# Wider gather blocks in a streaming MoE layer: three expert pairs to a block, one output column group per fill

## What is computed

```
for l in range(DEPTH):                      # 2 layers
    mix = hybrid_mixer(x, mem, ...)
    x = layer_norm(ALPHA * x + mix, ln1_g[l], ln1_b[l])
    top_idx, top_w = route(x, ...)          # 8 of 64 experts for each token
    y = sum over e: top_w * (silu(x @ w_gate[e]) * (x @ w_up[e])) @ w_down[e]
    x = layer_norm(ALPHA * x + y + swiglu(x, ws_gate, ws_up, ws_down), ln2_g[l], ln2_b[l])
```

## Time and profile before

| | us |
|---|---|
| median of 3 runs | 1224.52 (1223.61 to 1224.72) |
| the profiled execution, whole time | 1223.63 |
| its span, first to last instruction | 1221.7 |
| PE busy in the span | 1181.2 (97%) |
| DVE, ACT busy | 351.0 (29%), 262.0 (21%) |
| DMA | 452.45 MB, 370 GB/s over the span |

### The profile page before, as it was taken

How to read it: one execution, slowest core, us unless ns; L and a number is a source line. 1 busy time by engine, 2 the same in 40 slices (tenths; PEclk the granted TensorE clock), 3 DMA queues, 4 the chain that set the end, 5 groups by cost and what they waited for, 6 DMA issues and landing times.

```text
span 1221.7 us, 17928 instructions
## 1 busy us (share of the span) xinstructions
PE 1181.2 (97%) x7776; PEld 560.6 (46%) x7776; DVE 351.0 (29%) x1070; ACT 262.0 (21%) x509; POOL 10.4 (1%) x20
## 2 busy tenths in 40 slices
PE   7999899999999999999899999999999999999994
PEld 6764444444444444444386645344444443444431
DVE  0433632222222222222243337222222222222224
ACT  0132222221222212222112323122221222212210
POOL 0000000000000000000010000000000000000001
PEclk9999999999999999999999999999999999999998
DMA  9962299999999999999997415999999999999992
GB/s 384 421 285 83 87 392 430 427 426 428 427 427 426 426 428 428 426 427 426 422 387 308 192 35 206 399 429 427 428 426 427 427 428 428 427 426 426 429 427 107
DMA packets 35927, 452.45 MB, mean 370 GB/s; under 512 B 3969, under 2 KB 4097, under 8 KB 6529
## 3 DMA queue, kind: packets, MB, share of 16 engines
q1 hardware_dynamic: 35840, 451.22, 88.0%
HBM read 450.15 MB, written 1.05 MB: 369 GB/s over the span
## 4 chain that ended last, share of the span: by engine, by line
PE 89%; DMA 7%; DVE 2%; ACT 0%; POOL 0%; issue 0%; SPq 0%; POOLq 0%
PE bank L611 33%; PE bank L637 17%; PE bank L529 8%; PE bank L554 5%; PE bank L693 5%; PE bank L765 4%; DMA slots<-in_w_gu 3%; DMA slots<-in_w_dn 3%; PE bank L702 2%; PE bank L623 2%; PE bank L892 1%; PE bank L712 1%; PE bank L578 1%; PE bank L722 1%; PE bank L667 1%; PE bank L661 1%
## 5 line engine op out<-in xcount | busy, mean ns | idle before, releaser
L637 PE MATMUL bank<-slots,low 128*32 128x512 f32 x2048 | 233.0, 595 | 2.9 <-issue 1.7
L611 PE MATMUL bank<-slots,low 128*64 128x512 f32 x1024 | 226.5, 594 | 2.4 <-DMA slots<-in_w_gu 2.4
L611 PE MATMUL bank<-slots,xT 128*64 128x512 f32 x1024 | 226.1, 594 | 1.0 <-ACT xT L927 1.0
L1194 DVE SCALAR_TENSOR_TENSOR yparts<-bank,small,yparts 128x512 fp32r<-128x512 f32 x128 | 96.1, 751 | 249.7 <-ACT yparts L927 249.7
L529 PEld LDWEIGHTS bank<-high,low 128*128 128x128 bf16 x1536 | 108.2, 147 | 50.4 <-issue 49.7
L611 PEld LDWEIGHTS bank<-slots,low 128*64 128x64 f32 x1024 | 69.1, 137 | 132.4 <-issue 127.6
L611 PEld LDWEIGHTS bank<-slots,xT 128*64 128x64 f32 x1024 | 69.3, 137 | 130.6 <-issue 129.3
L927 ACT ACTIVATE yparts<-bank,small 128x512 fp32r<-128x512 f32 x128 | 88.0, 687 | 158.5 <-PE bank L637 158.5
L1186 DVE TENSOR_TENSOR high<-high,bank 128x256 f32<-128x256 f32 x64 | 26.9, 421 | 327.3 <-ACT high L949 327.3
L529 PE MATMUL bank<-high,low 128*128 128x128 bf16 x1536 | 117.7, 227 | 0.3
L637 PEld LDWEIGHTS bank<-slots,low 128*32 128x32 f32 x2048 | 60.6, 109 | 121.9 <-issue 116.6
(11 more groups left out here) (128 smaller groups left out, 664.3 us busy)
## 6 DMA issues: line engine op xcount, KB each, us to landing
slots<-in_w_gu SPq DMA_DIRECT2D x128, 2048.0 KB, 23.7
slots<-in_w_dn SPq DMA_DIRECT2D x64, 2048.0 KB, 23.2
slots<-in_dense SPq DMA_DIRECT2D x32, 1024.0 KB, 13.0
r<-in_pool_mat SPq DMA_DIRECT2D x2, 1024.0 KB, 23.6
r<-in_ln_g SPq DMA_DIRECT2D x4, 512.0 KB, 4.6
r<-in_ln_b SPq DMA_DIRECT2D x4, 512.0 KB, 5.6
slots<-in_shared_dn SPq DMA_DIRECT2D x2, 1024.0 KB, 4.9
low<-in_memt SPq DMA_DIRECT2D x2, 512.0 KB, 6.8
```

What stands on the lines that cost most here:

```text
L611: m = pe.matmul(H[64 * a:64 * a + 64, :], xg[B % 2][:, k, j, a, :], GU[g][:, a, :, k, :], start=k == 0, stop=k == KD - 1)
L637: m = pe.matmul(Y[half][r0:r0 + 32, :], hT[:, kc * P + 64 * a + 32 * t:kc * P + 64 * a + 32 * t + 32], DN[g][:, a, kc, half * 512:(half + ...
L1194: dve.scalar_tensor_tensor(ysp[:, 1, half * 512:(half + 1) * 512], Y[half][:, :], wslot[:, b:b + 1], ysp[:, 0, half * 512:(half + 1) * 512 ...
```

## The change

- A gather block is three pairs (`SPAN` = 3): 11 blocks, the last of two pairs. A fill is one output column group k (of 8): six matmuls of 192 columns (128 in the last block), each written as one run. Block B + 1 is filled in 3, 3 and 2 fills in the three pairs of block B. The third fill of a pair stands between the two halves of the down product (L637 before).
- ScalarE's copy of a fill is 384 columns (256 in the last block), and reads them in another order than they lie: token tile and place are swapped back during the copy.
- The first block of a layer takes 8 fills, 48 matmuls of 192 columns; fills 4 to 7 reuse banks 4 to 7 after ScalarE's copy of fills 0 to 3.
- `xg` now needs 3072 columns for each of its two buffers. The even one lies in the scratch area; the odd one lies in a joined tensor `xr` (`xT` and `r8`), and covers the first 1024 columns of `r8`. So the `ln2` loads are issued no longer before pair 2's weights but after the loop, once pair 29 has used the odd buffer, and ahead of the next layer's memt.
- `hT`, `pos` and `w3` move to memory that is free in the loop.

```
+SPAN = 3
+BLOCKS = -(-PAIRS // SPAN)
+WIDTH = [min(SPAN, PAIRS - SPAN * b) for b in range(BLOCKS)]
+FILLS = KD
...
-                sp.wait_ge(*x_at(l, 0, NT - 1))
-                norms(l, ln2_g, ln2_b)
                 sp.wait_ge(*full_at(l, "sh1"))
                 load_gu(main, l, 2, 2)
...
+                sp.wait_ge(main.h_full, l * PAIRS + PAIRS - 2)
+                norms(l, ln2_g, ln2_b)
...
-            def gather(ps, B, quarter, buf, to=G):
-
-                for kk in range(2):
-                    k = 2 * quarter + kk
-                    for t in range(NT):
-                        for s in range(3):
-                            m = pe.matmul(to[:].rearrange("p (k x t c) -> p k x t c", k=2, x=4, t=NT)[:, kk, :, t, :],
-                                          xsp[:, t, s, k::KD], sel[:, buf, t, :].rearrange("p (x c) -> p x c", x=4),
-                                          start=s == 0, stop=s == 2)
+            def gather(ps, B, k, buf, to=G):
+
+                x = 2 * WIDTH[B]
+                for t in range(NT):
+                    for s in range(3):
+                        m = pe.matmul(to[:, t * x * SLOTS:(t + 1) * x * SLOTS], xsp[:, t, s, k::KD], sel[:, buf, t, 0:x * SLOTS],
+                                      start=s == 0, stop=s == 2)
                 m.then_inc(ps.g_full, 1)
...
-                for f in range(4):
-                    gather(ps, first_block, f, 0, bank[4 + f])
-                pe.wait_ge(ps.g_sb, first_fill + 1)
+                for f in range(FILLS):
+                    if f >= 4:
+                        pe.wait_ge(ps.g_sb, first_fill + f - 3)
+                    gather(ps, 0, f, 0, bank[4 + f % 4])
+                pe.wait_ge(ps.g_sb, first_fill + 5)
...
+                    ks = [k for k in range(SPAN * j, SPAN * j + SPAN) if k < FILLS and filling]
...
                         m.then_inc(ps.y_full, 1)
+                        if half == 0 and len(ks) > 2:
+                            pe.wait_ge(ps.g_sb, fills + ks[2])
+                            gather(ps, B + 1, ks[2], (B + 1) % 2)
...
+                def g_fill(B, k, src=G):
+                    act.wait_ge(ps.g_full, first_fill + FILLS * B + k + 1)
+                    x = 2 * WIDTH[B]
+                    dst = xg[B % 2][:, k, 0:WIDTH[B]].rearrange("p r e (t c) -> p (r e) t c", t=NT)
+                    copy(dst, src[:, 0:NT * x * SLOTS].rearrange("p (t x c) -> p x t c", t=NT, x=x)).then_inc(ps.g_sb, 1)
```

More of the change, by code:

```diff
@@ L199, in build @@
         rt = pT[:, 0, :]
-        memT = [mixT, xT[:]]
+        memT = [mixT, xT]
         def prob_of(c):
@@ L208, in build @@
         off[0] -= NT * D
[L209 to L212, removed]
+        xg_even = part(KD * SPAN * P)
         off[0] += 2 * D + 2 * P
@@ L215, in build @@
         sg = part(2 * F).rearrange("p (t n) -> p t n", t=NT)
-        sel = part(2 * NT * P // 2, BF16).rearrange("p (b t c) -> p b t c", b=2, t=NT)
-        pos = part(NT * E)
+        sel = part(2 * NT * SPAN * 64 // 2, BF16).rearrange("p (b t c) -> p b t c", b=2, t=NT)
+        w3 = sg[:, 1, 0:NT * E * 3 // 2].bitcast(BF16).rearrange("p (t e s) -> p t e s", t=NT, s=3)
+        hT = sw[:, 0:2 * F]
+        pos = sw[:, 2 * F:2 * F + NT * E]
         off[0] = NT * 3 * D // 2 + D + KD * 2 * P
@@ L538, in turn_sel @@
                 gb = G[:].bitcast(BF16)
-                half = sel[:, q // 2 % 2, :, 64 * (q % 2):64 * (q % 2) + 64]
+                half = sel[:, q // SPAN % 2, :, 64 * (q % SPAN):64 * (q % SPAN) + 64]
                 for t in range(NT):
@@ L617, in body @@
                         pe.wait_ge(ps.selT_sb, n + 1)
-                        gather(ps, first_block + B + 1, 2 * j, (B + 1) % 2)
+                        gather(ps, B + 1, ks[0], (B + 1) % 2)
                     if not first:
@@ L625, in body @@
                     if filling:
-                        pe.wait_ge(ps.g_sb, fills + 1)
-                        gather(ps, first_block + B + 1, 2 * j + 1, (B + 1) % 2)
+                        pe.wait_ge(ps.g_sb, fills + ks[1])
+                        gather(ps, B + 1, ks[1], (B + 1) % 2)
                     pe.wait_ge(ps.w_in[2][g], (turn * USES[g] + use) * 16 + 16)
@@ L937, in run @@
                 base = turn * PAIRS
-                first_fill = turn * 4 * BLOCKS
-                def g_quarter(B, quarter, src=G):
-                    act.wait_ge(ps.g_full, first_fill + 4 * B + quarter + 1)
-                    dst = xg[B % 2][:, 2 * quarter:2 * quarter + 2].rearrange("p k r e s -> p (k r e s)")
-                    copy(dst, src[:, :]).then_inc(ps.g_sb, 1)
-                for f in range(4):
-                    g_quarter(0, f, bank[4 + f])
+                first_fill = turn * FILLS * BLOCKS
+                def g_fill(B, k, src=G):
[3 more added lines that the diff above has]
+                    copy(dst, src[:, 0:NT * x * SLOTS].rearrange("p (t x c) -> p x t c", t=NT, x=x)).then_inc(ps.g_sb, 1)
+                for f in range(FILLS):
+                    g_fill(0, f, bank[4 + f % 4])
                 def body(n, q, g, b, use, first, last):
+                    B, j = q // SPAN, q % SPAN
+                    ks = [k for k in range(SPAN * j, SPAN * j + SPAN) if k < FILLS and B + 1 < BLOCKS]
                     act.wait_ge(ps.h_full, n + 1)
                     act.activation(sg[:, 0, :], H[:, 0:F], ACT.Silu).then_inc(ps.silu_rd, 1)
-                    if q // 2 + 1 < BLOCKS:
-                        for f in range(2):
-                            g_quarter(q // 2 + 1, 2 * (q % 2) + f)
+                    for k in ks[0:2]:
+                        g_fill(B + 1, k)
                     act.wait_ge(ps.selT_sb, n + 1)
@@ L957, in body @@
                             .then_inc(ps.hi_rd, 1)
+                        if half == 0:
+                            for k in ks[2:]:
+                                g_fill(B + 1, k)
                 pairs_of_pass(base, body, 0, (lambda: load_count(act, l)) if round_ is None else None)
```

36 lines of the change are left out of this document (18 added, 18 removed).

## The result

The changed kernel takes 1232.05 us (1231.14 to 1233.13) against 1224.07 us (1223.58 to 1224.72) for the kernel before in the same comparison: a ratio of 1.0066, with a 95% interval of 1.0054 to 1.0078. The forecast of 1229.1 was 3 us short and the time lies just above the range of 1226.2 to 1231.8; slower was right, but in part by luck, as is said at the end of the point-by-point part. The profiled execution took 1232.54 us, its span was 1230.6, 8.9 more than before.

What follows compares the result with a forecast made beforehand. The DMA stream at 427 GB/s, 14.7 us a pair, was taken to bound the loops, not PE. First block 0.95 + 0.95 plus loads 2.7 made +4.6 us on 1224.5, so 1229.1 us, range 1226.2 to 1231.8.

Steps and rivals of the forecast that it cites:

- Part 1: Gathers inside the expert loop: 16 wide matmuls at 83 ns save PE about 0.3 us per pair, worth nothing on the path.
- 8 ns in a matmul at most: Loop gathers: writing contiguous columns instead of four runs of 32 saves at most 8 ns per matmul.
- Part 2: First block's gather ahead of pair 0: 48 wide matmuls, less a shorter last copy, net +0.95 us in each layer.
- The rival of slow permuted copies: First block: ScalarE's copies take 0.75 us instead of 0.5, giving +9.3 us, 1233.8; chance 8%.
- Part 3: Moved ln2 loads ahead of layer 1's dense: 2.9 us less 0.2 slack stalls L661, +2.7 us; hidden after layer 1.
- A later pair 0 is a later end, one for one: Loop start: the DMA stream starts with pair 0, so any delay of pair 0 delays the loop's end equally.
- The clock rival: Pairs from 22 on: PE's waits drop its clock to 1.2 GHz, giving 1240 us or more; chance 2%.
- The rival in which PE's pace counts: Expert loops: if the stream had room, filling pairs give 18 us, less the 4.6, so 1211; chance 5%.
- the waits from pair 22: Sign in the loop: from about pair 22 PE waits about 1.2 us per pair for w_gu and w_dn.
- the wait at the dense chunk: Sign after the loop: L661 of layer 1 waits nearly 3 us for the dense load.
- A: Post-measurement theory, loop: DMA held the kernel before by only 1.4 to 2.1 us a layer; finer cutting of PE's work costs more.
- B: Post-measurement theory, stream: the first block and moved norm loads delay the DMA stream; PE's slower pair is a side effect.

Runs made afterwards that it cites:

- the fused one: Changed kernel with the third fill's six matmuls directly behind the second's, in another PSUM bank, down product whole: 1226.79 us, ratio 1.0020.
- the two versions of the changed kernel with a fast PE: Changed kernel with the third fill's matmuls and copy left out, 1224.66 us; changed kernel with the third fill right behind the second, 1226.79 us.

## Why the prediction was right or wrong, point by point

**What bounds the kernel before: right, but with too little said of the margin.** The prediction said that PE's pace "has no more say once it is at or below 14.7 us a pair". A faster PE gives nothing (the kernel without the third fill; the fused one), and the 427 GB/s held in each kernel. But the bound of 14.7 is for an endless stream. PE starts with a lead and must be slower by only a little, over 30 pairs, for its own sum to end last: the waits at pair 31, worth 1.4 and 2.1 us, are the whole margin of a layer, 0.05 to 0.07 us per pair. A pair of 14.04 us, well below 14.7, was already too slow. The prediction had these numbers and used them for one direction only.

**Part 1: this step failed.** "PE gains about 0.3 us per pair, at most 0.4" rested on 16 x 83 ns, and no bound of it reached below zero; measured is a loss of 0.18. With it fell "It is worth nothing on the path": the loops lost 6.05 us where the sum has no term. Column time was right: back to back, a wide matmul takes 84 ns (4.05 us / 48 in the first block) for the 83 assumed. What was left out is what goes with a group. The fused kernel shows 12 in one group at 90 ns each (1.08 / 12), the changed one 6 at 109 to 122. Taking six out of the twelve costs 0.30 us: 0.15 for the group inside the down product, and 0.07 and 0.07 for a wait and the start behind it, since six before the down product cover less of VectorE's copy than twelve did. The prediction named that last effect, without a price. Cutting the down product adds 0.13. Why a group inside the down product takes 0.15 us more than one behind the transposes no run here separates. In a pair with three fills: 0.64 + 0.73 + 0.65 + 0.13 = 2.15 us, against 1.70 before, +0.45, as the chain's 14.31 for 13.86. In a pair with two: 0.64 + 0.72 = 1.36, less 0.34. Twice the one and once the other are +0.56 over three pairs, +0.18 a pair. The forecast average of 16 matmuls a pair was right, but it hid that two pairs of three pay for the third group. Nor is their width the cause: the kernel before with one quarter cut loses 0.54 us a pair with narrow matmuls.

**The layout, "8 ns in a matmul at most": wrong.** The saving from contiguous columns is none at 128 columns, by the kernel that writes in one run. The 62 ns of the earlier trace rows is the price of a 128-column matmul here in either layout.

**Part 2, the first block: right.** +0.92 and +0.91 for +0.95: the 48 matmuls take 159.81 to about 163.9, 4.05 us, and the last copy is shorter. The rival of slow permuted copies is refuted; ScalarE's copy of 384 columns takes 0.49 us (its timeline, changed kernel: duration after start):

```profile
160.51 3.96 ACT L933 ACTIVATE low<-bank 128x384 f32<-128x384 f32 x8 [5.37 <-PE bank L530]
...
172.29 0.49 ACT L933 ACTIVATE xr<-bank 128x384 f32<-128x384 f32 x1 [0.25 <-PE bank L530]
```

The first row also shows what the sum did not say: the eight copies run back to back, 0.495 us each, level with PE's fills of 0.506, and the chain of waits goes over the copies to pair 0. By that chain, slower copies would have lengthened this stretch; no run has them.

**Part 3, the loads: mechanism right, term mis-sized, and not on the path in the end.** "The slack is 0.2 us" was 1.2, because records were counted as matmuls; so the term is 1.75 in the kernel before, from start to start, and 1.1 to 1.15 in the two versions of the changed kernel with a fast PE. In the changed kernel itself it is zero, since PE comes to L667 after the data: the stretch is 143.96 us for 143.97.

**"A later pair 0 is a later end, one for one": right for a large shift, not seen for small ones.** Later by 3.0 came out as 2.9 a layer. Earlier by 0.6 came out as no gain in time. DMA had moved 403 GB/s for 400 in the 40 us from L578, about 0.3 us of stream. The landing of the last half scatters by about 1 us between kernels whose pair 0 starts alike (443.5 and 443.6 us after L578 in the kernel before, 444.5 and 443.3 with the gathers in one run), and with pair 0 later by 0.9 it came 0.3 earlier to 1.7 later. So shifts below 1 us can't be followed to the end in single traces, and whether something holds the stream besides pair 0 was not settled. In the changed kernel this does not matter: there pair 0's 0.9 us lie on PE's own path.

**The rivals.** The clock rival is refuted where its condition held: in the kernel without the third fill, with PE waiting up to 1.2 us per pair, PEclk is 1.00, that is 2.4 GHz, over 200 to 590. The rival in which PE's pace counts was close to the truth with the wrong sign. None of the rivals had PE slower inside the loop at the full clock, though the change cuts PE's work into more groups; that missing case is why the range ended at 1231.8. Of the signs named, the rate, the first block's 4 us and the copy came true; the waits from pair 22, the wait at the dense chunk and the late w_gu of pair 31 did not appear in the changed kernel. In the two versions with a fast PE the waits came later than pair 22 (from pair 24 and 23 without the third fill, from pair 28 of layer 0 with the fused one), the dense chunk did stall PE, and the last w_gu was late in three layers of four.

**What explains the 8.0 us.** A, with B's small part: 1.8 ahead of pair 0 and 6.05 in the loops, where 4.7 + 4.8 of PE time met waits worth 3.5. The kernel that differs only in where six matmuls stand gives 5.0 of it back, which shows A directly. That the forecast of slower held owes something to luck: of its 4.6 us, 2.7 cost nothing in the changed kernel, and most of the loss came from a stretch where it had expected none.

## What to carry to other kernels

Two bounds that differ by a wait of 1 us at the end of a 445 us loop are one bound: price an edit in both directions on both engines, since a gain is lost behind the one and a loss of more than 0.07 us per pair already shows. Where a change keeps the columns and alters how they are grouped, count the groups and the cuts, not only the columns, and ask for each group what it covers. And before a slack is read off a row, find out how many records of the trace one instruction of the code has.

## What the runs showed of the hardware that was not expected

- A group of six bfloat16 gathers inside a float32 product costs about 0.15 us more than the same six behind others: 0.65 us for 0.50 in the chain. With the wait that a shorter group uncovers, 12 of 192 columns take 1.08 us in one group and 1.38 in two; 12 of 128 take 0.83 in one and 1.25 in two, 1.06 of them without the 0.19 of waiting.
- A wait of PE in the middle of 32 float32 matmul records costs 0.2 us more than its row says: 8.37 us for 6.99 with a wait of 1.16.
- Cutting a group of sixteen float32 matmuls in two around such a group adds 0.13 to 0.14 us (3.57 to 3.70 or 3.71).
- PSUM writes in runs of 32 columns and in one run of 128 take the same time: 0.87 and 0.83 us against 0.88 and 0.84 for twelve.
- ScalarE's read of PSUM in permuted order takes 0.38 us for 256 columns and 0.49 for 384 (changed kernel); in order, 512 take 0.60. The three lie on one line, 0.11 us per 128 columns, so the order shows no price of its own.
